# A conditioned decoder step on Trainium2: the conditioning projection in whole groups of four weight units

## The reference, cut to what matters

```
def adaln(c, w, b):
    m = silu(c) @ w + b                      # w: 1024 x 9216 for each layer, c: 9 sequences
    return m.reshape(c.shape[0], N_SUB, 3, 1024)
# block s of a layer:
h = rmsnorm(x, g) * (1 + mod[:, s, 1]) + mod[:, s, 0]      # scale, shift
x = x + (0.5 or 1) * mod[:, s, 2] * block(h)               # gate
```

## Time and profile before

| | |
|---|---|
| median of 3 runs | 1357.04 us |
| profiled execution | 1356.68 us, its span 1354.9 us, mean granted clock 0.984 |
| TensorE (PE) busy | 1308.2 us, 97% of the span |
| VectorE (DVE) / ScalarE (ACT) / GpSimd (POOL) busy | 682.6 / 531.9 / 123.7 us |
| moved by DMA | 269.41 MB, 199 GB/s over the span |
| projection matmuls (L1149) | 1040 + 112 instructions |
| selecting matmuls (L1158) | 272 + 16 instructions |

### The profile page before, as it was taken

One profiled execution on the slowest core, in us unless ns is written; L12 is line 12 of the kernel. 1 busy time (PEld: TensorE's weight loads), 2 busy tenths in 40 slices (PEclk: granted clock), 3 DMA queues, 4 the chain that ended last, 5 costly groups with the idle time before them and its releaser, 6 DMA issues.

```text
span 1354.9 us, 25059 instructions
## 1 busy us (share of the span) xinstructions
PE 1308.2 (97%) x10405; PEld 1196.9 (88%) x10405; DVE 682.6 (50%) x1039; ACT 531.9 (39%) x730; POOL 123.7 (9%) x124
## 2 busy tenths in 40 slices
PE   6899999999999999999999999999999999999997
PEld 3799999999998999999899999998666579999996
DVE  0644444466666444444644444565645446545454
ACT  2534433243334444332544433244434325454331
POOL 4000001200030000012000001310011021000031
PEclk7899999999999999999999999999999999999998
DMA  9565656656664665566475654474246333444452
GB/s 358 206 238 213 229 197 221 240 201 238 242 237 156 243 224 212 207 227 227 186 278 195 240 198 163 167 291 142 109 164 257 124 114 122 174 161 177 130 169 78
DMA packets 41781, 269.41 MB, mean 199 GB/s; under 512 B 4785, under 2 KB 6257, under 8 KB 18273
## 3 DMA queue, kind: packets, MB, share of 16 engines
q1 hardware_dynamic: 29088, 176.18, 36.5%
q10 hardware_dynamic: 9440, 67.48, 13.1%
q0 software_dynamic: 3168, 24.52, 4.8%
HBM read 266.55 MB, written 1.62 MB: 198 GB/s over the span
## 4 chain that ended last, share of the span: by engine, by line
PE 92%; DVE 4%; DMA 1%; ACT 1%; issue 1%; POOL 0%; SPq 0%; DVEq 0%; ACTq 0%; POOLq 0%
PE bank L1110 26%; PE bank L1112 24%; PE bank L1111 24%; PE bank L1149 5%; PE bank L1335 3%; PE bank L1158 2%; PE bank L1385 1%; PE bank L1348 1%; DMA ada_early<-in_w_ada 1%; DVE rstd L768 1%; PE bank L1352 1%; PE bank L1117 1%; PE bank L1262 1%; PE bank L1266 1%; PE bank L1293 0%
## 5 line engine op out<-in xcount | busy, mean ns | idle before, releaser
L1110 PE MATMUL bank<-h_hi,w_hi 128*128 128x288 f32 x1712 | 514.7, 301 | 8.4 <-DVE h_lo L810 7.5
L734 DVE TENSOR_TENSOR w_lo<-stage,w_hi 128x2048 fp32r<-128x2048 f32 (+2 forms) x182 | 375.9, 2066 | 282.2 <-ACT w_hi L551 281.7
L1112 PE MATMUL bank<-h_hi,w_lo 128*128 128x288 f32 x1712 | 505.8, 295 | 0.0
L1111 PE MATMUL bank<-h_lo,w_hi 128*128 128x288 f32 x1712 | 505.6, 295 | 0.0
L551 ACT CAST w_hi<-stage 128x2048 fp32r<-128x2048 f32 (+2 forms) x182 | 304.6, 1674 | 135.7 <-PE bank L1112 123.0
L1110 PEld LDWEIGHTS bank<-h_hi,w_hi 128*128 128x128 f32 x1712 | 321.9, 188 | 27.3 <-issue 16.9
L1111 PEld LDWEIGHTS bank<-h_lo,w_hi 128*128 128x128 f32 x1712 | 322.2, 188 | 0.0
L1112 PEld LDWEIGHTS bank<-h_hi,w_lo 128*128 128x128 f32 x1712 | 321.9, 188 | 0.0
L1110 PE MATMUL bank<-gu_hi,w_hi 128*128 128x288 f32 x768 | 230.4, 300 | 0.0
L1111 PE MATMUL bank<-gu_lo,w_hi 128*128 128x288 f32 x768 | 226.6, 295 | 0.0
L1112 PE MATMUL bank<-gu_hi,w_lo 128*128 128x288 f32 x768 | 225.9, 294 | 0.0
(11 more groups left out here) (198 smaller groups left out, 956.8 us busy)
## 6 DMA issues: line engine op xcount, KB each, us to landing
stage<-in_w_gu SPq DMA_DIRECT2D x88, 1024.0 KB, 4.8
stage_ada<-in_w_ada ACTq DMA_DIRECT2D x64, 1024.0 KB, 5.4
stage<-in_w_down SPq DMA_DIRECT2D x64, 704.0 KB, 4.1
stage<-in_w_ci SPq DMA_DIRECT2D x16, 768.0 KB, 5.8
ada_early<-in_w_ada SPq DMA_DIRECT2D x7, 1024.0 KB, 14.4
stage<-in_w_co SPq DMA_DIRECT2D x4, 1024.0 KB, 6.8
stage<-in_w_wo SPq DMA_DIRECT2D x4, 1024.0 KB, 4.9
stage<-in_w_mi SPq DMA_DIRECT2D x3, 1024.0 KB, 4.8
```

The costliest lines, as they stand in the source:

```text
L734: nc.vector.tensor_tensor(w_lo[part][:, 0:cols], stage[st_][:, 0:cols], w_hi[part][:, 0:cols], ALU.subtract).then_inc(lo_ready, 1)
L1110: nc.tensor.matmul(out, hi, x_hi, start=start, stop=False)
L1111: nc.tensor.matmul(out, hi, x_lo, start=False, stop=False)
L1112: return nc.tensor.matmul(out, lo, x_hi, start=False, stop=stop)
```

## The change

The projection is done in 18 groups of four units (1024 features, 4 MB).

- **In a group** each of the four column tiles takes one unit of its own and runs over all 8 contraction tiles: 32 matmuls of 256 columns, the same number as four units had. Bank 6 then holds finished sums, four units in four groups of 32 partitions. There is one copy to `ada_tok`, two transposes with `ident` in place of the selecting matmuls, and one VectorE addition that writes 8 tiles of `mods`. `mod_ready` counts groups: 3 n + 2 for the coefficients, 3 n + 3 for the gate.
- **Loads.** A group comes in four quarters of two contraction tiles, 1 MB each in runs of 2 KB, into a ring of four buffers: `stage_ada` and three in the region. TensorE waits for each quarter. When a whole group is used, ScalarE issues the four loads of the next (L561 four times). Groups 0 and 1 are loaded by the sync queue at the start (x after the first quarter, the first weight unit before the last two quarters of group 1), group 1 into buffers of its own. The load of group 2 is issued when group 0 is used.
- **Places.** Group 0 is `ada_first`, group 1 `ada_second`. Twelve stand in the stretches, late in each: before the fifth of six gu units in every iteration of ffn0, ffn1 and ffn2 (nine), one in ffn2's rest, two in conv_in; the transposes one unit later. Four stand between blocks (norm1 to norm4), none between attention and ffn3. The down, conv_out and mla_out stretches have none.
- **Between blocks** TensorE runs half of the group before the statistics and half behind them, instead of the dummy matmuls, which stay at norm 5 only. ScalarE loads the next group and copies the bank after its last h_hi, and the transposes and VectorE's addition come after the next block's first weight unit.
- **The rest.** The convolution's buffers move in the region; `u_sample` is loaded by GpSimd's queue after block 0's last residual instead of at the start, and its first columns are cleared before conv_in. GpSimd's loads for the attention also wait for the last group.

```diff
 def with_ada(units, n):
+    gap, out = len(units) // n if n else 0, []
     for j, unit in enumerate(units):
+        if n and j % gap == gap - 2 and j // gap < n:
+            out.append(Unit("ada"))
         out.append(unit)
-        if pending:
+        if n and j % gap == gap - 1 and j // gap < n:
             out.append(Unit("asum"))
...
-PLAN = ([Segment("ada_first", 1, ada_ahead(ADA_FIRST - 2)), Segment("ada_second", 1, ada_ahead(2))]
-        + gu_segments(0, True) + down_segments(0, 0, 3, 1) + between(1)
+PLAN = ([Segment("ada_first", 1, [Unit("ada"), Unit("asum")]), Segment("ada_second", 1, [Unit("ada"), Unit("asum")])]
+        + gu_segments(0, 1) + down_segments(0, 0) + between(1)
         + conv_segments() + between(2)
-        + gu_segments(1, True) + down_segments(1, 2, 3, 1) + between(3)
-        + gu_segments(2, True) + down_segments(2, 3, 0, 1) + between(4)
-        + mla_segments() + between(5)
-        + gu_segments(3, False) + down_segments(3, 5, 0, 0))
+        + gu_segments(1, 1) + down_segments(1, 2) + between(3)
+        + gu_segments(2, 1, 1) + down_segments(2, 3) + between(4)
+        + mla_segments()
+        + gu_segments(3, 0) + down_segments(3, 5))
...
+        def quarter(n, q):
+            units = a["w_ada"][C_TILES * n:C_TILES * (n + 1)] if isinstance(n, int) else \
+                a["w_ada"][bass.ds(C_TILES * n, C_TILES), :, :]
+            return units.rearrange("g p (q n) -> p g q n", q=RING)[:, :, q, :]
...
-            for j in range(ADA_FIRST - 1):
-                sp.dma_start(ada_early[j][:].rearrange("p k n -> p (k n)"), a["w_ada"][j]).then_inc(early_loaded[j], 16)
-                if j == 1:
+            for q in range(RING):
+                sp.dma_start(by_run(ring[q]), quarter(0, q)).then_inc(ada_loaded[q], 16)
+                if q == 0:
                     sp.dma_start(x[:], a["x"]).then_inc(x_in, 16)
-                if j == ADA_FIRST - 3:
+            for q in range(RING):
+                sp.dma_start(by_run(ada_early[q]), quarter(1, q)).then_inc(early_loaded[q], 16)
+                if q == 1:
                     sp.dma_start(stage[0][:, 0:FLAT[0]], a["w_gu"][0]).then_inc(loaded[0], 16)
...
             for n in range(MLA_BLOCK):
                 squares(n)
-                if n == 0:
+                if n == 1:
+                    pool.wait_ge(x_ready, KT)
                     pool.dma_start(u_sample[:, :, :, 0:CONV_WIDTH - 1], a["state"]).then_inc(state_in, 16)
...
             def load_ada(j):
-                act.dma_start(stage_ada[:].rearrange("p k n -> p (k n)"), src).then_inc(ada_loaded, 16)
+                for q in range(RING):
+                    act.dma_start(by_run(ring[q]), quarter(j, q)).then_inc(ada_loaded[q], 16)
...
                 if n:
                     nc.scalar.activation(any_root[:], eps[:], ACT.Sqrt)
-                    after(between_steps(act, n)[0])
                     root(n)
                 for kt in range(KT):
...
+                if n and between_step(act, n):
+                    after(between_step(act, n))
...
                 if st.kind == "asum":
                     dve.wait_ge(asum_done, st.place + 1)
...
+                    summed = bank[7][:, 0:2 * P].rearrange("p (h g c) -> p h g c", h=2, g=C_TILES)[:, :, :, 0:NC_]
+                    nc.vector.tensor_tensor(
+                        group_of(mods, st.place).rearrange("p (g h) c -> p h g c", h=2), summed,
+                        group_of(bias, st.place).rearrange("p (g h) -> p h g", h=2).unsqueeze(3)
+                        .broadcast_to([P, 2, C_TILES, NC_]), ALU.add).then_inc(mod_ready, 1)
...
             def stats(n):
-                ada = between_steps(pe, n) if 0 < n < DEPTH * N_SUB else ()
+                ada = between_step(pe, n) if n else None
                 if ada:
-                    products(ada[0])
+                    ada_products(ada, range(0, RING // 2))
...
                 if ada:
-                    products(ada[1])
+                    ada_products(ada, range(RING // 2, RING))
+                elif 0 < n < DEPTH * N_SUB:
                     keep_busy(N_WARM, 5)

+            def ada_products(st, quarters):
+                for q in quarters:
+                    if isinstance(st.place, int) and st.place == 1:
+                        weights = ada_early[q]
+                        pe.wait_ge(early_loaded[q], 16)
+                    else:
+                        weights = ring[q]
+                        pe.wait_ge(ada_loaded[q], 16 * max(1, st.place) if isinstance(st.place, int) else 16 * st.place)
+                    for kk in range(2):
+                        for g in range(C_TILES):
+                            mm = nc.tensor.matmul(bank[6][C_PAD * g:C_PAD * (g + 1), 0:2 * P], silu_c[:, 2 * q + kk, :],
+                                                  weights[:, g, kk, :], start=q == 0 and kk == 0,
+                                                  stop=q == RING - 1 and kk == 1)
+                if quarters[-1] == RING - 1:
+                    mm.then_inc(ada_used, 1)
...
                     for m in range(2):
-                        mm = nc.tensor.matmul(bank[7][:, NC_ * m:NC_ * (m + 1)], tok_of(st)[0][:, P * m:P * (m + 1)],
-                                              select[:, 0:NC_], start=True, stop=True)
+                        mm = nc.tensor.transpose(bank[7][:, P * m:P * (m + 1)], ada_tok[:, P * m:P * (m + 1)], ident[:])
                     mm.then_inc(asum_done, 1)
```

More of the change, by code:

```diff
@@ L108, in with_ada, with gu_segments @@
 def with_ada(units, n):
-    out, left, pending = [], n, 0
+    gap, out = len(units) // n if n else 0, []
     for j, unit in enumerate(units):
+        if n and j % gap == gap - 2 and j // gap < n:
+            out.append(Unit("ada"))
         out.append(unit)
-        if pending:
+        if n and j % gap == gap - 1 and j // gap < n:
             out.append(Unit("asum"))
-            pending = 0
-        if left and (j % 2 == 0 or left > (len(units) - j) // 2):
-            out.append(Unit("ada"))
-            left, pending = left - 1, 1
-    assert not left
-    return out + [Unit("asum")] * pending
-def gu_segments(f, ada):
+    return out
+def gu_segments(f, ada, ada_rest=0):
     def gu(m, step, banks):
@@ L893, in after, with run @@
                     convolve(st)
-            def run(name):
-                for st in steps(dve, SEG[name], split=True):
+            def run(name, asum=None):
+                for st in steps(dve, SEG[name], split=True, peel_first=asum is not None):
                     split_ahead(st)
                     after(st)
+                    if asum is not None:
+                        after(asum)
+                        asum = None
             nc.vector.memset(ones[:], 1.0).then_inc(setup_done, 1)
             nc.vector.memset(eps[:], EPS).then_inc(setup_done, 1)
-            nc.vector.memset(u_prompt[:, :, 0:CONV_WIDTH - 1], 0.0).then_inc(setup_done, 1)
             dve.wait_ge(consts_in, 16)
@@ L1205, in run @@
                     products(st, h_from if first or st.kind == "ci" and st.tile == 0 else None)
+                    if first and asum is not None:
+                        products(asum)
                     first = False
```

151 lines of the change are left out of this document (69 added, 82 removed).

## The result

The changed kernel takes **1321.86 us** (median of 4 runs, 1320.09 to 1323.36), the kernel before 1356.95 us in runs of the same session (4 runs, 1355.97 to 1358.17): ratio 0.974, with a 95% interval of 0.972 to 0.976. The profiled execution took 1323.36 us, its span 1321.6 us; that is 33.3 us less than the span before.

The account below looks back on a forecast made before the run. TensorE's instruction stream, plus the start and the gaps between blocks, was taken to bound the kernel. From 1356.7 us profiled, -46.2 + 2.6 + 5.6 + 0.4 + 4.0 = -33.6 gave 1323 us, range 1309 to 1336.

Parts of the forecast that it names:

- the main: The forecast itself, for the whole kernel: 33.6 us less, 1323 us, chance 0.56.
- The stream: units: TensorE's stretches: 59 units of 1.19 us become 12 groups of 3.83 us, 24.2 us less.
- Rival (c): Every group: column tiles stop overlapping, rounds take 0.44 us instead of 0.22, 47 us more, 1370; chance 0.04.
- The stream: sums: TensorE's stretches: 58 sums of 0.44 us become sixteen transpose pairs of 0.22 us, 22.0 us less.
- wait for the copy: After the first conv unit, TensorE's transposes wait for ScalarE's copy behind four loads: 0.4 us more (0 to 1.8).
- Between blocks: Norms 1, 3 and 4: half a group makes the statistics 0.87 us later each, 2.6 us more; hidden at norm 2.
- clock: Behind the four gaps at norms 1 to 4: granted clock falls, 1.4 us each, 5.6 us more (0 to 10).
- The start: Before the first block: early loads share queues with group 2's, landing 38.5, coef 42.3, 4.0 us more (-2.8 to +7.2).
- Rival (a): Start and norm gaps: early loads keep pace and the clock survives, 1311; one alone 1316 to 1317; chance 0.22.
- Rival (b): Norms 1, 2 and 3: quarters for conv_in's seventh and gu's fifth unit 3 us late, +9, 1332; chance 0.15.
- Rival (d): TensorE's stream: weight splits bind, the gain turns into waits for w_lo, 1357 within 3; chance 0.03.

Follow-up runs that it names:

- Experiment 3: The changed kernel with each of its twelve groups in the stretches cut in two halves, one weight unit apart: 1329.86 us.
- experiment 8: The changed kernel with w_ada laid out by quarters, one run of 8 KB a partition instead of four of 2 KB: 1323.49 us.
- Experiment 7: The changed kernel with ScalarE's copy of the bank ahead of its four ring loads instead of behind: 1316.91 us.
- experiment 6: The changed kernel with one quarter of the group ahead of the statistics and three behind, instead of two and two: 1318.43 us.
- experiment 5: The changed kernel with group 2's four ring loads issued after ScalarE's last h_hi of block 0 instead of at the use of group 0: 1316.75 us.
- 9: The changed kernel with ScalarE's copy ahead of the four ring loads and 10 dummy matmuls behind the group's second half at norms 1 to 4: 1319.03 us.
- 4: The changed kernel with 10 dummy matmuls behind the second half of the group at norms 1 to 4: 1321.25 us.
- experiment 12: The kernel of experiment 11 with w_ada in runs of 8 KB instead of 2 KB: 1311.31 us.
- experiment 1: The kernel before with one selecting matmul of 18 columns a unit instead of two of 9, leaving out the second 128 features: 1346.21 us.
- 10: The changed kernel with copy first, one quarter before the statistics and three behind, group 2's loads behind norm 0, unit 1's cast ahead of it: 1311.79 us.
- experiment 11: The kernel of experiment 10 with 6 dummy matmuls behind the three quarters: 1308.61 us.
- experiment 2: The kernel before without the dummy matmuls at norms 1 to 4; norm 5 keeps them: 1364.60 us.

## Why the prediction was right

The mechanism was as put in the main, and the sum came to within 0.3 us of the span's change; that closeness is luck in part, since terms of both signs were off by up to 1.8 us and the profiled execution was the slowest of its four (by the medians the sum is 1.5 us short).

- **The stream: units.** 3.79 us for 3.83 forecast, and rounds of 0.22 throughout. Experiment 3 shows the fixed price of 0.33 us by itself. The forecast went from 59 units to 12 groups in one step and didn't say that more than half of its 24 us are units that leave the stretches for the gaps; gathering alone is worth 12. Rival (c) falls: all 1088 instructions average 395 ns, against 386. The 0.8 us beyond the forecast are 12 x 0.04 and the rounding of a unit to 1.19 us (59 of them took 70.5, not 70.2).
- **The stream: sums.** The choice of 0.22 between ends of 0.11 and 0.44 was right where nothing waits. Mis-sized: the **wait for the copy**. I took four issues of 0.345 us, the median of single loads of 8 KB rows, 1.4 in all. They took 2.5 us, so TensorE waited 0.9 us at norm 1 and not 0.4, and 0.7 at norm 2, where I had the copy covered by a longer unit: 1.7 us together. The upper end of 1.8 held it. The short runs are the smaller part of the error: with 8 KB runs four issues in a row still took 2.1 us (experiment 8). Why four in a row cost more than four single ones is open. Experiment 7 removes the waits.
- **Between blocks.** 0.8 to 1.0 us each at norms 1, 3 and 4 for 0.87 forecast, and experiment 6 takes it away. At norm 2 the gap became 0.5 us shorter. At norm 5 it is 9.17 us as before: TensorE waits 2.65 us for GpSimd instead of 1.30, and a fall of the clock that came right behind (1094.6 to 1098.0) ran out inside the gap. The **clock**: I took a fall at each of four gaps and 1.4 us for each. It fell at three; they cost 1.5, 2.4 and 1.5 us, and a start that was cold for longer 0.5. The sum is near, the parts are not.
- **The start.** 2.5 us for 4.0: the last quarter landed at 37.3, not 38.5, coef followed in 3.6 us as put. With the ring out of the way it lands at 31.6 (experiment 5); my 31.8 for that case was right, and the sharing cost 5.7 us where I took 6.7. The two queues in the changed kernel from 22 to 37 us (packets, MB, share of 16 engines):

```profile
DMA packets 2519, 6.21 MB, mean 414 GB/s; under 512 B 92, under 2 KB 92, under 8 KB 2319
...
q1 hardware_dynamic: 1321, 3.81, 63.1%
q10 hardware_dynamic: 1197, 2.39, 41.0%
```

  At 414 GB/s the ring's 2.39 MB are 5.8 us: the late quarter pays for what the ring moves ahead of it, and that was 38% of the bytes, not an even half. By the limit of about 358 GB/s a core, which the page reckons as half of an HBM stack's rate for each of two cores (the Trainium skill, DMA: Bandwidth & Descriptors, Specifications), the start would have cost an estimated 5.4 us; the trace of this kernel on one core doesn't agree, with 414 GB/s over 15 us and a start of 2.5 us.
- **What was not in the sum.** The attention took 1.8 us more. Over all traces here it takes 149.0 to 149.3 us with no fall of the clock in it, 150.5 to 150.7 with one of 3.4 us, and 152.3 to 153.7 with two or a longer one. What decides whether it falls there isn't settled; no edit here touches the block.
- **Rival (a)** didn't come: the early loads were late, and the clock fell behind three of the four norms. The experiments show what its two parts are worth: 5.7 us at the start (5), and 3.7 to 4.0 us of weight time at the norms (9 and 4). **Rival (b)**: no wait for w_lo or late quarter in the changed kernel, so its margin was enough; experiment 12 shows waits of that kind for weights, 4.6 us, once the ring's runs are long. **Rival (c)** fell with the rounds. **Rival (d)** fell with experiment 1.

## What to carry to other kernels

Work interleaved with a bound stream can pay a fixed price each time it switches in, here 0.33 us: put it in fewer, longer pieces (12 us here). And where the engine idles or runs dummies anyway, real work may be nearly free: 11 units that moved there were worth another 13 us, less 2 us on the gaps and 5.4 to the clock. Before moving a piece ahead of a statistic or filling a gap, ask what follows on the slower engine: here half of a group and one copy behind four load issues gave back 4 us, and a load issued 20 us too early cost the start 5.7. In experiment 12 a background load with longer runs took more of the queues from an urgent one: short runs can be the better choice for it.

## What the runs showed that I had not expected

- **Issuing loads can hold an engine.** Four loads of 1 MB in 2 KB runs took ScalarE's queue 7.21 us at the start, while both hardware queues were full; behind the norms of the changed kernel they took 2.4 to 2.5 us, and in the stretches up to 4.6. In 8 KB runs they took 1.85 us at the start, 2.0 to 2.1 behind the norms and up to 3.7 in the stretches (experiment 8).
- **The idle that costs the clock** has no sharp length in these traces. Of the idles ahead of a block at norms 1 to 4 over all traces of this study, a fall of the clock began in it or within 1.5 us behind it in 4 of 4 at 4.67 us, 17 of 20 at 3.15 us, 3 of 6 at 2.3 us, and none of 26 at 1.6 us or less. Norm 2 of the changed kernel is one of the three of 3.15 us that stayed warm. The idle counted here is only that ahead of the block: at norm 2 TensorE also waits for GpSimd inside the gap, and a fall began within 1 us behind such a wait of 1.97 us in four traces (before, experiments 1, 6 and 10) and not in experiment 11; in experiment 2 it can't be told from the one of 4.67. Whether an earlier stretch decides it is open.
- **Kept clock isn't always kept gain**: the dummies of experiments 4 and 9 saved 3.7 to 4.0 us of weight time and the attention was 1.3 and 4.7 us slower in the same executions; in experiment 11 it was not.
